# A two-block transformer kernel on one core: rotary angles, layer constants and half of x are moved to other engines and places in the start-up

## The reference

```python
for layer in range(DEPTH):                      # 2 layers
    h = rms_norm(x, norm_w[layer])
    proj = h @ w_in[layer]
    (q, k, v, z_attn, q_h, f_h, i_h, g_h, gate_attn, gate_hgrn) = jnp.split(proj, split_points, axis=-1)
    q = partial_rope(q.reshape(B, T, N_HEADS, HEAD_DIM), positions)      # cos and sin of positions * inv_freq
    k = partial_rope(k.reshape(B, T, N_KV_HEADS, HEAD_DIM), positions)
    a = sliding_window_attention(q, k, v, attn_sinks[layer]).astype(x.dtype) * jax.nn.silu(z_attn)
    lb = lb_all[layer]                          # from a softmax of lb_logits over the layers
    logf = jnp.log(lb + (1.0 - lb) * jax.nn.sigmoid(f_h))
    kin = (1.0 - lb) * jax.nn.sigmoid(-f_h)
    o = hgrn2_recurrence(silu(q_h), kin, i_h, logf)
    b = norm(o) * jax.nn.silu(g_h)
    merged = sigmoid(gate_attn) * (a @ w_up_attn[layer]) + sigmoid(gate_hgrn) * (b @ w_up_hgrn[layer])
    x = x + merged @ w_out[layer]
```

## Time and profile before

| | us |
|---|---|
| three runs | 839.87, 838.94, 840.10 |
| median | 839.87 |
| profiled execution, its own time | 839.87 |
| its span, from the first to the last instruction | 838.1 |
| TensorE busy | 813.0 (97%) |
| DVE busy | 597.9 (71%) |
| ScalarE busy | 479.1 (57%) |
| GpSimd busy | 27.2 (3%) |

### The profile page before, as it was taken

How to read it: one execution, slowest core, us unless ns; L and a number is a source line. 1 busy time by engine, 2 the same in 40 slices (tenths; PEclk the granted TensorE clock), 3 DMA queues, 4 the chain that set the end, 5 groups by cost and what they waited for, 6 DMA issues and landing times.

```text
span 838.1 us, 13421 instructions
## 1 busy us (share of the span) xinstructions
PE 813.0 (97%) x5162; PEld 732.2 (87%) x5162; DVE 597.9 (71%) x698; ACT 479.1 (57%) x557; POOL 27.2 (3%) x59
## 2 busy tenths in 40 slices
PE   8989999999999999999999999999979999999977
PEld 7978899998989889999888999999877788888866
DVE  6789765768589787577657557557679877787872
ACT  6874775433786576453477444443468666665661
POOL 7100000000000000300000000000000000000000
PEclk9999999999999999999999999999989999999999
DMA  8345434365436633366635535465039979797901
GB/s 279 127 152 200 151 118 135 113 204 187 127 128 201 201 101 113 111 192 180 208 110 174 165 101 156 168 204 177 1 94 371 310 270 345 265 321 279 331 24 50
DMA packets 70481, 149.72 MB, mean 179 GB/s; under 512 B 8506, under 2 KB 11920, under 8 KB 70416
## 3 DMA queue, kind: packets, MB, share of 16 engines
q1 hardware_dynamic: 70000, 148.78, 53.3%
q0 software_dynamic: 384, 0.04, 0.1%
q10 hardware_dynamic: 32, 0.01, 0.0%
HBM read 147.76 MB, written 1.05 MB: 178 GB/s over the span
## 4 chain that ended last, share of the span: by engine, by line
PE 77%; DVE 11%; ACT 5%; issue 4%; DMA 2%; SPq 0%; DVEq 0%; ACTq 0%
PE mm L599 9%; PE mm L601 9%; PE mm L600 9%; PE mm L583 8%; PE mm L584 8%; PE mm L585 8%; PE aux L1047 4%; PE aux L1045 4%; PE aux L1046 4%; DVE sb_w_lo L1590 4%; PE aux L779 3%; PE aux L687 2%; PE aux L720 2%; PE aux L742 1%; DVE sb_gb L1590 1%
## 5 line engine op out<-in xcount | busy, mean ns | idle before, releaser
L1590 DVE TENSOR_TENSOR sb_w_lo<-sb_raw,sb_w_hi 128x2048 fp32r<-128x2048 f32 (+2 forms) x150 | 318.5, 2134 | 60.0 <-ACT sb_w_hi L1453 28.9
L1157 ACT ACTIVATE sb_w_hi<-sb_raw 128x2048 fp32r<-128x2048 f32 (+1 forms) x86 | 160.8, 1873 | 169.2 <-PE mm L601 116.0
L599 PE MATMUL mm<-sb_hT_hi,sb_w_hi 128*128 128x256 f32 x592 | 170.2, 287 | 2.4 <-DVE sb_hT_lo L1691 1.7
L601 PE MATMUL mm<-sb_hT_hi,sb_w_lo 128*128 128x256 f32 x592 | 167.4, 283 | 0.0
L600 PE MATMUL mm<-sb_hT_lo,sb_w_hi 128*128 128x256 f32 x592 | 167.4, 283 | 0.0
L1453 ACT ACTIVATE sb_w_hi<-sb_raw 128x2048 fp32r<-128x2048 f32 x50 | 95.9, 1919 | 39.5 <-PE aux L1047 17.0
L599 PEld LDWEIGHTS mm<-sb_hT_hi,sb_w_hi 128*128 128x128 f32 x592 | 113.4, 192 | 4.5 <-issue 2.2
L583 PE MATMUL mm<-sb_w_hi,sb_hT_hi 128*128 128x512 f32 (+1 forms) x288 | 111.7, 388 | 3.3 <-DVE sb_w_lo L1590 3.3
L600 PEld LDWEIGHTS mm<-sb_hT_lo,sb_w_hi 128*128 128x128 f32 x592 | 113.5, 192 | 0.0
L601 PEld LDWEIGHTS mm<-sb_hT_hi,sb_w_lo 128*128 128x128 f32 x592 | 113.4, 192 | 0.0
L584 PE MATMUL mm<-sb_w_lo,sb_hT_hi 128*128 128x512 f32 (+1 forms) x288 | 109.6, 381 | 0.0
(11 more groups left out here) (397 smaller groups left out, 1370.6 us busy)
## 6 DMA issues: line engine op xcount, KB each, us to landing
sb_raw<-in_w_in SPq DMA_DIRECT2D x120, 512.0 KB, 4.5
sb_raw<-in_w_down SPq DMA_DIRECT2D x32, 512.0 KB, 6.0
sb_raw<-in_w_gate SPq DMA_DIRECT2D x31, 512.0 KB, 5.0
sb_raw<-in_w_up SPq DMA_DIRECT2D x31, 512.0 KB, 6.8
sb_raw<-in_w_out SPq DMA_DIRECT2D x16, 512.0 KB, 4.5
sb_raw<-in_w_up_attn SPq DMA_DIRECT2D x8, 512.0 KB, 4.3
sb_raw<-in_w_up_hgrn SPq DMA_DIRECT2D x8, 512.0 KB, 4.4
sb_raw<-in_w_o SPq DMA_DIRECT2D x8, 512.0 KB, 4.6
```

The source lines that it names most:

```text
L599: pe.matmul(dst, w[0][:, k, cs], acts[0][:, k, :], start=start, stop=False, skip_group_check=True)
L601: return pe.matmul(dst, w[1][:, k, cs], acts[0][:, k, :], start=False, stop=stop, skip_group_check=True)
L1157: act.activation(w_hi[:, slot(t), 0:width], raw[:, slot(t), 0:width], ACT.Copy).then_inc(hi_split, 1)
L1590: return dve.tensor_tensor(out_, a, b, op)
```

## The change

Seven things are changed, all of them in the start-up of layer 0 or in what is passed over in layer 1.

1. `rope_angles` leaves GpSimd. DVE runs it, in layer 0 only, behind loop step 1, so between the low part of tile 3 and `f_clamp`. The arithmetic is the same.
2. `later_gains` is gone. What it did is in `bounds`, which makes the constants of both layers.
3. The second half of x is issued by ScalarE once the first half has landed, and no longer by SP between tiles 0 and 1.
4. GpSimd's two small loads (sinks, one gain) are issued ahead of the attention masks, without a wait for x.
5. DVE takes the first gain out of PSUM ahead of `level_masks`.
6. TensorE waits for `half_lo` ahead of the whole body of a layer's tile 0, and so ahead of `first_products`.
7. The fillers `keep_busy` are 4, 3 and 6 where they were 8, 2 and 9.

```diff
@@ SP
                     load(i, halves(i, B1_TILES[i], layer), layer * NT1 + i)
-                    if i == 0:
-                        with sp.If(layer < 1):
-                            load_x(sp, 1)
@@ GpSimd
             load_rows(pool, rows[1:], in_rows)
+            pool.dma_start(lcols_all[:, :, LAYER_COLS - 8:], A["attn_sinks"].partition_broadcast(P)).then_inc(in_sinks, 16)
+            pool.dma_start(ffn_gain[:], A["ffn_norm_g_2"].rearrange("(p k) -> p k", k=KT)).then_inc(S["ffn_gain_in"], 16)
...
-            pool.wait_ge(in_x[1], 16)
-            pool.dma_start(lcols_all[:, :, LAYER_COLS - 8:], A["attn_sinks"].partition_broadcast(P)).then_inc(in_sinks, 16)
-            rope_angles()
-            pool.dma_start(ffn_gain[:], A["ffn_norm_g_2"].rearrange("(p k) -> p k", k=KT)).then_inc(S["ffn_gain_in"], 16)
@@ TensorE, use_tile
                 if first_half is None:
                     pe.wait_ge(lo_split, sofar + (RING + 1))
+                else:
+                    pe.wait_ge(S["half_lo"], first_half)
                 body(tile_parts(t, n, width)).then_inc(tile_done, 1)
@@ TensorE, start
             pe.wait_ge(S["ident_ready"], 1)
-            keep_busy(8)
+            keep_busy(4)
             pe.wait_ge(in_norm_w, 16)
...
-            keep_busy(2)
+            keep_busy(3)
             pe.wait_ge(in_x[0], 16)
             x_transposes((1, 1), 0, None)
-            keep_busy(9)
+            keep_busy(6)
@@ ScalarE
             act.activation(hst[:, 31:32], one[:, 1:2], ACT.Copy)
+            act.wait_ge(in_x[0], 16)
+            load_x(act, 1)
@@ DVE
+            def rope_angles():
+
+                inv_freq = [float(np.float32(np.power(np.float32(500000.0), np.float32(-i * (2.0 / 16))))) for i in range(8)]
+                dve.wait_ge(in_pos, 16)
+                hold(dve.tensor_copy(st[:, 56:58], pos_i[:]))
+                for i in range(8):
+                    ins = ts_(rope_t[:, 0, :, i], st[:, 56:58], inv_freq[i], ALU.mult)
+                hold(ins)
+                hold(ts_(rope_t[:, 1], rope_t[:, 0], 1.0 / (2 * np.pi), ALU.mult))
+                hold(ts_(rope_t[:, 1], rope_t[:, 1], 12582912.0, ALU.add))
+                hold(ts_(rope_t[:, 1], rope_t[:, 1], 12582912.0, ALU.subtract))
...
+                for c in (part1, part2, part3):
+                    hold(ts_(rope_t[:, 2], rope_t[:, 1], c, ALU.mult))
+                    hold(tt_(rope_t[:, 0], rope_t[:, 0], rope_t[:, 2], ALU.subtract))
+
+                hold(ts_(rope_t[:, 4], rope_t[:, 0], np.pi / 2, ALU.add))
+                hold(ts_(rope_t[:, 3], rope_t[:, 4], float(np.pi), ALU.is_gt, 2 * np.pi, ALU.mult))
+                hold(tt_(rope_t[:, 4], rope_t[:, 4], rope_t[:, 3], ALU.subtract))
+                hold(dve.tensor_copy(rope_t[:, 5], rope_t[:, 0]))
+                top = 3.1415925
+                hold(ts_(rope_t[:, 4:6], rope_t[:, 4:6], top, ALU.min, -top, ALU.max))
+                dve.sem_inc(S["rope_in"], 1)
...
-            level_masks()
             dve.wait_ge(S["setup_pe"], 1)
             link(dve.tensor_copy(gain[:], mm[1][:, 0:KT]))
             dve.sem_inc(S["gain_now"], 1)
+            level_masks()
...
             def bounds():
...
-                tt_(lower, hst[:, 0:4], hst[:, 20:24], ALU.mult)
-                hold(tt_(lower_next, hst[:, 4:8], hst[:, 20:24], ALU.mult))
-                tt_(lcols_all[:, 0, 0:4], lower, lower, ALU.subtract)
-                dve.tensor_copy(lcols_all[:, 0, 8:9], cols[:, COL_AT["hgrn"]:COL_AT["hgrn"] + 1])
-                hold(dve.memset(lcols_all[:, 0, 4:8], 1.0))
-                hold(tt_(lcols_all[:, 0, 4:8], lcols_all[:, 0, 4:8], lcols_all[:, 0, 0:4], ALU.subtract))
...
+                hold(ts_(one[:, 2:3], cols[:, COL_AT["q_gain"]:COL_AT["q_gain"] + 1], 0.125, ALU.mult))
+                dve.wait_ge(S["lb_exp"], 1)
+                hold(tt_(hst[:, 16:20], hst[:, 0:4], hst[:, 4:8], ALU.add))
+                hold(dve.reciprocal(hst[:, 20:24], hst[:, 16:20]))
+                tt_(hst[:, 0:4], hst[:, 0:4], hst[:, 20:24], ALU.mult)
+                hold(tt_(hst[:, 4:8], hst[:, 4:8], hst[:, 20:24], ALU.mult))
+                hold(tt_(hst[:, 8:12], hst[:, 0:4], hst[:, 4:8], ALU.add))
+                for layer in range(2):
+                    dve.tensor_copy(lcols_all[:, layer, 8:9], cols[:, COL_AT["hgrn"] + layer:COL_AT["hgrn"] + layer + 1])
+                    src = hst[:, 0:4] if layer == 0 else hst[:, 8:12]
+                    hold(tt_(lcols_all[:, layer, 0:4], src, hst[:, 0:4], ALU.subtract))
+                    hold(ts_(lcols_all[:, layer, 4:8], lcols_all[:, layer, 0:4], -1.0, ALU.mult, 1.0, ALU.add))
                 dve.wait_ge(in_sinks, 16)
...
                         layer_low(i + 2)
-                    if i == 9:
+                    if i == 1:
                         with dve.If(L < 1):
-                            later_gains()
+                            rope_angles()
```

46 lines of the change are left out of this document (5 added, 41 removed).

## The result

| | before | after |
|---|---|---|
| median, us | 839.58 (838.32 to 840.10) | 847.78 (846.37 to 848.45) |
| profiled execution, us | 839.87 | 848.2 |
| its span, us | 838.1 | 846.5 |

The ratio is 1.0098, with a 95% interval of 1.0085 to 1.0110: 8.2 us slower. The forecast was 845.5 in a range of 843.0 to 848.0. The sign held, and so did the mechanism of the two largest terms; the sum of 5.6 was 2.6 too small. Of the signs that the prediction gave for itself, the angles' time, the gaps ahead of tiles 4 and 5 and tile 5's start before 52 us came true. One of its signs of being wrong came true too: r is made more than 1 us away from 23.87. And every later row stands 7.3 to 7.9 us late, not 5 to 6.

What follows compares the result with a forecast made beforehand. Until 44.83 us DVE and ScalarE were taken to bound the kernel, from there TensorE. The terms 1.0 + 4.0 + 0 + 0 + 0.6 + 0 = 5.6 us on 839.87 gave 845.5 us, range 843.0 to 848.0.

Steps and rivals of the forecast that it cites:

- What bounds the kernel: Start-up: until tile 5's matmul at 44.83 us DVE and ScalarE set the time; delays there reach the end in full.
- Part 1: DVE ahead of tile 3: eight instructions moved into bounds cost 1.0 us, between 0.9 and 1.15.
- Part 2: DVE between tile 3's low part and rB: the 23 rope_angles instructions cost 4.0 us, between 3.4 and 4.9.
- Rival C: Start-up: DVE's rope code and bounds are hidden, so not slower, at best 838.6 us; chance 0.04.
- Part 3: Start-up loads: x's second half on ScalarE's queue and two earlier GpSimd transfers change nothing, 0 us.
- rival A: Start-up loads: tile 1 lands 1.3 us earlier because SP's queue goes first, giving 844.2 us; chance 0.16.
- Part 4: TensorE's start: it begins at 10.8, 1.2 us late, but spare time absorbs this: 0, up to 0.9 us.
- rival B: TensorE's start: its lateness gets through, making DVE's columns and r 0.9 us late, 846.4 us; chance 0.12.
- Part 5: TensorE's clock at tile 5: a longer gap ahead lengthens the lower-clock stretch, 0.6 us, between 0 and 1.2.
- Layer 1: The layer's same chain, now with a branch past the rope code: 0 us, upper end 0.5.
- Rival D: Rope code or its branch also costs layer 1 0.5 us or more, or held instructions cost 0.27: 846.9 us; chance 0.10.

Runs made afterwards that it cites:

- e1: The changed kernel with the rotary angles back on GpSimd, behind the attention masks; ratio to the kernel before 1.0045.
- e12: The kernel before with only GpSimd's two small loads issued early, ahead of the masks and without waiting for x; ratio to the kernel before 1.0018.
- e6: The changed kernel with GpSimd's two small loads late again, behind the masks and x; x's second half stays on ScalarE; ratio to the kernel before 1.0080.
- e7: The changed kernel with x's second half issued by SP between tiles 0 and 1 again, small loads still early; ratio to the kernel before 1.0102.
- e3: The changed kernel with both orders of loads as before (x's second half on SP, GpSimd's small loads late); ratio to the kernel before 1.0097.
- e2: The changed kernel with TensorE's start as before: fillers 8, 2 and 9, first products not waiting for the low part; ratio to the kernel before 1.0094.
- e8: The kernel before with only the longer bounds, making the constants of both layers, and later_gains gone; ratio to the kernel before 1.0038.
- e10: The changed kernel with the angles still on DVE, but behind loop step 5 instead of 1; ratio to the kernel before 1.0064.
- e5: The kernel before, unchanged, profiled a second time; the kernel before had a median of 838.91 us in that series.
- e11: The kernel before with fewer constants made on DVE ahead of tile 3: layer 0's by memsets, other bounds work moved later; ratio to the kernel before 1.0001.
- e9: The kernel before with the longer bounds added and later_gains kept, writing the same values again; ratio to the kernel before 1.0015.

## Why the prediction was right, and where it fell short

The measured time lies 0.2 us inside the upper end of the range. It got there with two terms that the sum had at 0, the small loads and the start of layer 1.

**What bounds the kernel** held: from tile 1's landing through r, rB, the scan and tile 5's low part every link of the chain shifted by what had been added up to it, and TensorE by 6.34 us. Removing `later_gains` at 76 us gave nothing: the shift is 7.25 us on both sides of it.

**Part 1**, 1.0: measured 1.05, and in the two profiles that have it alone 1.06 and 1.07. **Part 2**, 4.0: measured 4.02; by the times of the change and of e1, 4.4. The durations of 4 elements carried over to 16. **Rival C** is dead: the sigmoids slipped with DVE, from 31.27 to 37.63.

**Part 3** is the step that failed, in the half sentence "The two GpSimd transfers that start earlier are of 4 and 8 KB: nothing". They were sized by their bytes. They cost 1.28 us in the profile of the changed kernel (1.4 to 3.3 us of tile 1's landing in the profiles that have them early), and 1.5 us in time when done alone (e12, 0.5 to 2.5); taking them away (e6) gave as much, within the intervals. The trace names one of the two, the sinks. The part that was argued at length, x's half on another queue, was right with 0: e6 and e7 separate it. In **rival A** tile 1 was to land earlier, and it landed 1.39 us later.

**Part 4** gave 0, and 0 it was, but with luck in the working. TensorE started at 12.61 and not at 10.8: with fewer fillers it stood idle for 1.12 us until the norm rows landed, and then made x's eight transposes in 1.91 us for 1.04, half the pace (the granted clock of these rows reads 1.00 all the same), which delayed ScalarE's first high part from 6.96 to 8.46. That is not so every time: the same start of TensorE gave 10.46 to 12.61 in the six profiles that have it, and 10.46 in e6, without the idle time. Its block with the transposes of the norm rows ended at 20.66 and not at 17.6, which left DVE's column copy waiting for 0.30 us, of which it would have lost 0.23 in any case. That is all that was left of the spare time, and **rival B** was that near. e3 (TensorE at 11.51, r at 23.23) and e2 (9.85, r at 26.45) show that it did not decide.

**Part 5**, 0.6: measured 0.9, from 6.34 at tile 5's first matmul to 7.25 at 59.28. That the value is near is luck: the reasoning took one profile's lower-clock stretch as a property of its gap. The second profile of the kernel before has the same gap of 2.35 and no such stretch, and measured from it the term is 2.5 us (the change is 6.93 us late at tile 5's first matmul and 9.45 at 59.28). e1 and e8 have gaps of 3.41 and 3.42, e1 with no stretch and e8 with one from 46 to 49 us; e10 has one of 6.8 us behind a gap of 3.20. Only the gap of 5.4 us was followed by the same, 6.8 us, in all four profiles that have it. For the shorter gaps a term for the clock is worth plus or minus 1.6 us, what the stretch of the earlier trace rows cost.

**Layer 1**, 0 with 0.5 as the upper end: measured 0.6. The branch that was priced costs nothing (rB follows tile 3's low part in layer 1 at once, 238.51 behind 236.30). The loss stands at the loop's second pass, where DVE begins 2.98 us behind ScalarE's high part (227.50 to 230.48) and not 2.47 as before (220.23 to 222.70), by 'issue', so by nothing that the profile shows:

```profile
230.48 1.66 DVE L1680 SCALAR_TENSOR_TENSOR sb_hT_lo<-aux,sb_gain,sb_hT_hi 128x256 fp32r<-128x256 f32 x4 [5.39 <-issue]
```

It is in every profile but the two of the kernel before. What it depends on is open; in this case it came with any edit that was run, also one of GpSimd's program alone (e12). **Rival D** had its 0.5 us at the start of layer 1, but not the cause, and the held instructions cost 0.21 us, not 0.27.

**The rest**, 0.5 us, is 2.1 lost at 640 to 660 us and 1.6 won at 810 to 815 us. The second is not of the change: e5 wins the same in the kernel before. The first is not seen in e5 at that place. From 598 us to the last block the profiles lose up to 1.6 us (e11) and win up to 2.4 (e12) against the first profile, so that 0.5 is no term of the change; what sets it is open.

The account by the profile: 1.28 + 1.05 + 4.02 + 0.9 + 0.6 + 0.5 = 8.35, of which 5.6 was forecast. By the times of the experiments, angles 4.4, small loads 1.5, bounds 1.3 (e9): 7.2 of the 8.2 measured, with an uncertainty of 2 to 3.
